# Two of four gate weight slots computed as Strassen block products inside the attention units

## The reference, cut to what matters

```python
q, k, v, qi, ki, wi, u, ga, gb = jnp.split(xn @ w_in, cuts, axis=-1)      # ga, gb: 1024 columns each
m = jax.nn.sigmoid(ga) * (attn_o @ w_branch_attn) + jax.nn.sigmoid(gb) * (pool_o @ w_branch_pool)
h = x + m @ w_out
h = h + moe_ffn(rms_norm(h, ffn_norm_g), ...)                              # 32 experts, top 2
```

## Time and profile before

| what | us |
|---|---|
| median of 3 runs | 1079.64 |
| lowest, highest run | 1079.25, 1081.33 |
| span of the profiled execution (first to last instruction) | 1078.2 |
| PE busy in the span | 948.8 |
| DVE busy | 338.8 |
| ACT busy | 201.7 |
| POOL busy | 196.8 |

### The profile page before, as it was taken

How to read it: one execution, slowest core, us unless ns; L and a number is a source line. 1 busy time by engine, 2 the same in 40 slices (tenths; PEclk the granted TensorE clock), 3 DMA queues, 4 the chain that set the end, 5 groups by cost and what they waited for, 6 DMA issues and landing times.

```text
span 1078.2 us, 12247 instructions
## 1 busy us (share of the span) xinstructions
PE 948.8 (88%) x4745; PEld 534.2 (50%) x4745; DVE 338.8 (31%) x756; ACT 201.7 (19%) x446; POOL 196.8 (18%) x296
## 2 busy tenths in 40 slices
PE   7989999999999999999998999888888877877870
PEld 6644444777676566774553544424334243432420
DVE  3269999965441111330135000000000000000016
ACT  3143110223343334001121000000000000000012
POOL 2740650100001200000231112201111111111122
PEclk9999999999999999999999999999899999999995
DMA  9920211430203832934038999999999999999986
GB/s 341 395 97 1 78 57 68 153 149 18 79 1 138 265 145 69 359 153 156 40 131 322 423 424 422 423 419 426 423 422 424 422 426 421 425 425 423 418 341 208
DMA packets 53690, 283.82 MB, mean 263 GB/s; under 512 B 8684, under 2 KB 9552, under 8 KB 33031
## 3 DMA queue, kind: packets, MB, share of 16 engines
q1 hardware_dynamic: 42807, 246.24, 57.0%
q0 software_dynamic: 10784, 36.97, 9.4%
q10 hardware_dynamic: 56, 0.01, 0.0%
HBM read 267.41 MB, written 23.17 MB: 270 GB/s over the span
## 4 chain that ended last, share of the span: by engine, by line
PE 55%; DMA 26%; DVE 3%; ACT 2%; issue 2%; SPq 1%; POOL 0%; POOLq 0%; ACTq 0%; DVEq 0%
DMA arena<-in_w_exp_up 24%; PE psum L788 11%; PE psum L957 6%; PE psum L626 5%; PE psum L975 5%; PE psum L1063 4%; PE psum L1060 4%; PE psum L1061 4%; PE psum L1080 3%; PE psum L909 1%; DMA y_d<-arena 1%; PE psum L875 1%; PE psum L837 1%; PE psum L859 1%; PE psum L999 1%
## 5 line engine op out<-in xcount | busy, mean ns | idle before, releaser
L1063 PE MATMUL psum<-arena 128*64 128x512 f32 x704 | 164.1, 619 | 28.9 <-DMA arena<-in_w_exp_up 28.2
L1080 PE MATMUL psum<-arena 128*64 128x512 f32 x512 | 116.9, 597 | 17.7 <-ACT arena L1365 17.7
L788 PE MATMUL psum<-arena 128*128 128x288 f32 x480 | 124.6, 412 | 0.0
L1063 PEld LDWEIGHTS psum<-arena 128*64 128x64 f32 x704 | 54.8, 143 | 136.2 <-issue 101.6
L788 PEld LDWEIGHTS psum<-arena 128*128 128x128 f32 x480 | 88.4, 190 | 30.3 <-issue 8.1
L1734 DVE TENSOR_TENSOR arena<-arena,psum 128x256 f32<-128x256 f32 x32 | 13.5, 421 | 274.7 <-ACT arena L1361 274.7
L1361 ACT ACTIVATE arena<-psum 128x256 f32<-128x256 f32 x32 | 12.3, 383 | 402.8 <-PE psum L1063 270.5
L626 PE MATMUL psum<-arena 128*128 128x512 f32 x192 | 84.5, 594 | 0.2 <-ACT arena L1232 0.2
L1080 PEld LDWEIGHTS psum<-arena 128*64 128x64 f32 x512 | 40.4, 136 | 72.1 <-issue 71.4
L1060 PE MATMUL psum<-arena 128*64 128x256 f32 x320 | 56.8, 413 | 15.3 <-DMA arena<-in_w_exp_up 15.3
L1742 DVE COPY arena<-psum 128x512 f32<-128x512 f32 x31 | 21.4, 692 | 152.2 <-PE psum L1080 152.2
(11 more groups left out here) (291 smaller groups left out, 1090.0 us busy)
## 6 DMA issues: line engine op xcount, KB each, us to landing
arena<-in_w_exp_down SPq DMA_DIRECT2D x32, 2048.0 KB, 36.9
arena<-in_w_exp_gate SPq DMA_DIRECT2D x29, 2048.0 KB, 32.3
arena<-in_w_exp_up SPq DMA_DIRECT2D x19, 2048.0 KB, 37.2
arena<-in_w_exp_up SPq DMA_DIRECT2D x26, 1024.0 KB, 33.4
arena<-in_w_in SPq DMA_DIRECT2D x7, 2048.0 KB, 8.8
y_d<-arena SPq DMA_DIRECT2D x1, 8192.0 KB
arena<-in_w_exp_gate SPq DMA_DIRECT2D x6, 1024.0 KB, 13.9
arena<-in_x_prompt SPq DMA_DIRECT2D x8, 512.0 KB, 8.2
```

The source lines that it names most:

```text
L788: last = pe.matmul(bank(2 + n % 2 if n < SAMPLE_G else 2, HN), ring[slot % 2][:, k, m * P:(m + 1) * P], xnT[:, k, HN * hh:HN * hh + HN], s ...
L1063: last = pe.matmul(bank(2 + s, 512, rows).rearrange("p (w n) -> p w n", w=2), x_k, wgu[j][:, :, DE * k + 256 * q:DE * k + 256 * q + 256], ...
L1080: last = pe.matmul(bank(4 + s, 512, slice(64 * half, 64 * half + 64)), hT[s][:, k % 2, CAP * (k // 2):CAP * (k // 2) + CAP], wd[j][:, k, 5 ...
```

## The change

Slots 4 and 5 (gate products 8 to 23, 16 products of 8 matmuls) are computed in another way. A slot's 1024 by 512 weights are taken as pairs of 128-column blocks (`lo`, `hi`), each with an upper and a lower half of the 1024 rows; the tokens as a left and a right half. Each pair is one 2 by 2 block product, done with seven block products of 4 matmuls in place of eight (Strassen's scheme in its form with 15 sums). There are four such pairs (`q` = 0 to 3), so 28 products `g` of 4 matmuls. The sums of weight quarters (`asum`, 4 for each pair, 512 columns; one of them written over the slot itself) and of input quarters (`tsum`, 4 in all, 1152 columns) are made by POOL. `fast_product` issues a product into bank 2 or 3 by turns, and some products accumulate onto what their bank holds from an earlier one. `take_fast` on DVE copies out or adds each result, 28 in place of 16.

In units 0 and 1 PE issues gate products 6 and 7 as before; in units 2 to 15 it issues two fast products in a row at the place of the one gate product, and DVE takes the two of unit u-1 in its round `u`, at the place of the one copy. The numbering of fills is f = n below 8, f = 8 + g for the fast ones, and 36 to 43 for gate products 24 to 31, which now fill the eight places in the sample stage. Nothing is left of the gates behind attention, so the branch products come first there. The sigmoids run in another order, and DVE waits for them tile by tile. POOL makes the input sums and the first weight sums before its first gather of keys, the other three sets of weight sums between it and the first gather of values, and that gather waits for `g_done` 36 (the end of the fast products), because `vb` shares its space with the sums. A slot of `ring` is free again after 8, 22, 36, 44, 60 and 76 products.

```diff
+        gb_raw = [at(ZB - 2 * NT, NT), at(MP, NT), at(ZB - NT, NT), at(GAR + 4 * NT, NT)] + [at(QZ + k * NT, NT) for k in range(4)]
+        assert NT <= 5 * P and GAR + 5 * NT <= MP and QZ + 4 * NT <= KT1
+        QUAD = 4 * HN
+        tsum = [at(ZB + 4096 + j * QUAD, 4, HN) for j in range(3)] + [at(ZB + 8192, 4, HN)]
+        asum = {1: at(SMALL, 4, P), 2: at(where["expand"][0], 4, P), 4: at(ZB + 4096 + 3 * QUAD, 4, P)}
...
-        RING_USED = [(S["jp"], v) for v in (10, 15, 20)] + [(S["g_done"], v) for v in (8, 16, 24, 32, 48, 64)]
-
-        PRE, SAMPLE_G = 6, 22
-        EARLY = SAMPLE_G + DB
-        assert PRE <= 8 and EARLY <= 32 and EARLY - 16 <= 2 * len(gb_raw)
+        RING_USED = [(S["jp"], v) for v in (10, 15, 20)] + [(S["g_done"], v) for v in (8, 22, 36, GATES, GATES + 16, GATES + 32)]
+
+        PRE, SAMPLE_G = 6, 24
+        assert PRE <= 8 and SAMPLE_G + DB == 32
+
+        def fill_of(n):
+            return n if n < 8 else FILLS + n - SAMPLE_G
+
+        def fast_places(g):
+            q, step = g // 7, g % 7
+            slot, pair = R_GATES + 1 + q // 2, q % 2
+            tiles = sgA[4:8] if q < 2 else gb_raw[0:4]
+            return slot, pair, step, tiles[pair], tiles[2 + pair]
...
+                f = fill_of(n)
...
-                    if n >= 2:
-                        pe.wait_ge(S["raw_ev"], n - 1 if n <= SAMPLE_G else n)
+                    if f >= 2:
+                        pe.wait_ge(S["raw_ev"], f - 1 if n <= SAMPLE_G else f)
...
+            def fast_product(g):
+
+                slot, pair, step, _, _ = fast_places(g)
+                f, w = 8 + g, ring[slot % 2]
+                lo, hi = slice(pair * P, pair * P + P), slice((2 + pair) * P, (3 + pair) * P)
+                left, right = slice(0, HN), slice(HN, NT)
+                if step == 0:
+                    ring_ready(slot)
+                if step == 1:
+                    pe.wait_ge(S["sums_t"], 1)
+                    pe.wait_ge(S["sums_a"], 2 * (g // 7) + 1)
+                if step == 6:
+                    pe.wait_ge(S["sums_a"], 2 * (g // 7) + 2)
+                pe.wait_ge(S["raw_ev"], f - 1)
+                a, b = ((w[:, 0:4, lo], xnT[:, 0:4, left]), (asum[2], tsum[1]), (w[:, 4:8, lo], xnT[:, 4:8, left]), (w[:, 0:4, hi], tsum[2]),
+                        (asum[1], tsum[0]), (w[:, 4:8, hi], tsum[3]), (asum[4], xnT[:, 4:8, right]))[step]
+                for k in range(4):
+                    last = pe.matmul(bank(2 + f % 2, HN), a[:, k, :], b[:, k, :], start=(k == 0 and step in (0, 1, 4)), stop=(k == 3), skip_group_check=True)
+                last.then_inc(S["g_done"], 1)
...
-                    gate_part(PRE + u, 0, KD)
+                    if PRE + u < 8:
+                        gate_part(PRE + u, 0, KD)
+                    else:
+                        for g in (2 * (PRE + u - 8), 2 * (PRE + u - 8) + 1):
+                            fast_product(g)
...
-            for p3 in range(3):
-                slot = R_GATES + 3 + p3
+            n = 0
+            for p3 in range(2):
+                slot = R_GATES + 4 + p3
...
-                        if p3 == 0:
-                            b = g_bank()
-                            for k in range(KD):
-                                last = pe.matmul(bank(b, HN), w[:, k, m * P:(m + 1) * P], xnT[:, k, tc], start=(k == 0), stop=(k == KD - 1))
...
-            act.wait_ge(S["raw_ev"], EARLY)
+            act.wait_ge(S["raw_ev"], GATES)
             act.wait_ge(S["son_done"], DB // 2)
-            for k in range(len(gb_raw)):
+            act.activation(sgA[0], sgA[0], ACT.Sigmoid).then_inc(S["gs_done"], 1)
+            for k in range(KD):
                 act.activation(sgB[k], gb_raw[k], ACT.Sigmoid).then_inc(S["gs_done"], 1)
-            for k in range(KD):
+            for k in range(1, KD):
                 act.activation(sgA[k], sgA[k], ACT.Sigmoid).then_inc(S["gs_done"], 1)
-            for n in range(EARLY, 32):
-                act.wait_ge(S["g_done"], n + 1)
-                act.activation(sgB[(n - 16) // 2][:, HN * (n % 2):HN * (n % 2) + HN], bank(4 + (n - EARLY) % 4, HN), ACT.Sigmoid).then_inc(S["gate_ev"], 1)
...
+            def take_fast(g):
+
+                _, _, step, upper, lower = fast_places(g)
+                left, right = slice(0, HN), slice(HN, NT)
+                if g == 0:
                     dve.wait_ge(S["rope_done"], len(JOBS))
                     for s in range(2):
                         dve.wait_ge(s_rs[s], stored[s])
-                dve.wait_ge(S["g_done"], n + 1)
-                dst = sgA[4 * (n // 8) + m] if n < 16 else gb_raw[(n - 16) // 2]
-                dve.tensor_copy(dst[:, cols_h], bank(2 + n % 2 if n < SAMPLE_G else 2, HN)).then_inc(S["raw_ev"], 1)
+                dve.wait_ge(S["g_done"], 8 + g + 1)
+                src = bank(2 + g % 2, HN)
+                if step == 0:
+                    ins = dve.tensor_copy(lower[:, left], src)
+                elif step == 2:
+                    ins = dve.tensor_copy(upper[:, left], src)
+                else:
+                    dst, old = ((upper[:, right], lower[:, left]), None, (lower[:, right], lower[:, left]), (lower[:, right], lower[:, right]),
+                                (lower[:, left], lower[:, left]), (upper[:, right], upper[:, right]))[step - 1]
+                    dve.wait_ge(S["raw_ev"], 8 + g)
+                    ins = dve.tensor_tensor(dst, src, old, ALU.add)
+                ins.then_inc(S["raw_ev"], 1)
...
-                    take_gate(PRE + v)
+                    if PRE + v < 8:
+                        take_gate(PRE + v)
+                    else:
+                        for g in (2 * (PRE + v - 8), 2 * (PRE + v - 8) + 1):
+                            take_fast(g)
...
-                dve.wait_ge(S["gs_done"], KD + len(gb_raw))
-                if mg:
-                    dve.wait_ge(S["gate_ev"], 32 - EARLY)
                 for m in range(4):
+                    dve.wait_ge(S["gs_done"], 1 + len(gb_raw) + 4 * mg + m)
...
+            def left_sums(q):
+
+                slot, pair = R_GATES + 1 + q // 2, q % 2
+                w = ring[slot % 2]
+                lo, hi = slice(pair * P, pair * P + P), slice((2 + pair) * P, (3 + pair) * P)
+                if q:
+                    pool.wait_ge(S["g_done"], 8 + 7 * (q - 1) + 5)
+                pool.wait_ge(s_ring[slot % 2], RING_AT[slot])
+                link(pool.tensor_tensor(asum[1], w[:, 0:4, hi], w[:, 4:8, hi], ALU.add))
+                pool.tensor_tensor(w[:, 0:4, hi], w[:, 0:4, lo], w[:, 0:4, hi], ALU.subtract)
+                pool.tensor_tensor(asum[2], asum[1], w[:, 0:4, lo], ALU.subtract).then_inc(S["sums_a"], 1)
+                if q:
+                    pool.wait_ge(S["g_done"], 8 + 7 * q)
+                pool.wait_ge(S["sums_a"], 2 * q + 1)
+                pool.tensor_tensor(asum[4], w[:, 4:8, lo], asum[2], ALU.subtract).then_inc(S["sums_a"], 1)
+
+            x11, x12, x21, x22 = (xnT[:, 4 * kh:4 * kh + 4, HN * nh:HN * nh + HN] for kh in range(2) for nh in range(2))
+            link(pool.tensor_tensor(tsum[0], x12, x11, ALU.subtract))
+            pool.tensor_tensor(tsum[2], x22, x12, ALU.subtract)
+            link(pool.tensor_tensor(tsum[1], x22, tsum[0], ALU.subtract))
+            pool.tensor_tensor(tsum[3], x21, tsum[1], ALU.subtract).then_inc(S["sums_t"], 1)
+            left_sums(0)
             for bp in range(DB // 2):
                 if bp:
                     pool.wait_ge(S["tp"], T0 + 32 + 11 * (bp - 1) + 8)
@@ -1897,6 +1958,10 @@
                     gather(kb[:, b2, :], k_groups, gidx[:, 2 * bp + b2:2 * bp + b2 + 1], s_kin[b2])
                 if bp:
                     pool.wait_ge(S["spv_done"], bp)
+                else:
+                    for q in range(1, 4):
+                        left_sums(q)
+                    pool.wait_ge(S["g_done"], FILLS)
                 for b2 in range(2):
                     gather(vb[:, b2, :], v_groups, gidx[:, 2 * bp + b2:2 * bp + b2 + 1], s_vin[b2])
                 if bp == 0:
```

More of the change, by code:

```diff
@@ L277, in program @@
         sgA = [at(BANDS + k * NT, NT) for k in range(4)] + [at(GAR + k * NT, NT) for k in range(4)]
-        gb_raw = [at(ZB - 2 * NT + k * NT, NT) for k in range(2)] + [at(MP, NT)] + [at(QZ + k * NT, NT) for k in range(4)]
-        assert NT <= 5 * P
+        gb_raw = [at(ZB - 2 * NT, NT), at(MP, NT), at(ZB - NT, NT), at(GAR + 4 * NT, NT)] + [at(QZ + k * NT, NT) for k in range(4)]
[3 more added lines that the diff above has]
+        asum = {1: at(SMALL, 4, P), 2: at(where["expand"][0], 4, P), 4: at(ZB + 4096 + 3 * QUAD, 4, P)}
+        assert 3 * QUAD + 4 * P <= 4096 and where["expand"][1] >= 4 * P and QUAD <= 2 * LS
         pgi = arena[0:DB, XNT - 80:XNT - 80 + NPAGE].bitcast(I32)
@@ L392, in program @@
         OV, N0 = M[0], NE // 2
+        FILLS = 8 + 28
+        GATES = FILLS + 8
         RING_LOADS = [w_in_v[:, :, c:c + 512] for c in (C_Q, C_K, C_U)]
@@ L488, in _ @@
             load_ring(8)
```

(36 more changed lines are left out.)

4 lines of the change are left out of this document (2 added, 2 removed).

## The result

The changed kernel takes 1124.29 us (median of 4 runs, 1123.86 to 1126.53) against 1080.04 before (4 runs, 1079.25 to 1081.33). The ratio is 1.0412, 95% interval 1.0400 to 1.0425, so 44.3 us slower. The profiled execution is the slowest of the four runs (1126.53); its span is 1125.0 us, 46.8 more than before, so what follows from its rows comes out some 2 us above the medians.

What follows compares the result with a forecast made beforehand. PE's own stream was taken to bound the prompt units, and weight DMA the expert stage. -7.8 + 35 + 10.9 = +38 on the span of 1078.2 gave 1116, with the runs' offset 1117.7, stated as 1117 us; range 1105 to 1127.

Steps and rivals of the forecast that it cites:

- the likeliest case (A): Prompt units: all terms as summed, clock falling after 4 to 13 gaps; 1113 to 1128 us, chance 0.60.
- Term 1: Behind attention: the last two gate products, 32 matmul records, go from PE's path; -7.8 us.
- so term 1 stands whole: Behind attention: sigmoids, DVE and weight loads keep ahead of the branch products, so the full 7.8 us is gained.
- Term 2: Units 3 to 15: PE waits for DVE to empty a PSUM bank, 13 gaps; +35 us.
- Term 3: Prompt units: PE's clock falls after long gaps, 1.66 us a fall; +10.9 us, bounds 0 and 21.6.
- I take falls in the last eight at 9 of 11: Units 8 to 15: clock falls at the expert stage's rate for long waits, 8 x 0.82 x 1.66 us.
- The upper bound of 21.6: Prompt units: a clock fall of 1.66 us after each of the 13 gaps.
- PE's work in the units is denser: Prompt units: PE's other work is denser than in the expert stage, given for the lower bound of 0 falls.
- POOL's sums and the gathers: Prompt stage: POOL's additions and the moved gathers stay hidden behind other work; cost 0.
- Case C: Prompt units: another wait on top, late values or weight sums, or POOL slowing DVE; 1128 to 1140 us, chance 0.07.
- B: Prompt units: the gaps come but the clock stays, up to 3 falls; 1106 to 1112 us, likeliest 1107, chance 0.26.
- D: Prompt units: not slower, gaps below 0.60 us a unit; down to 1072 us, chance 0.05 faster, 0.02 tie.

Runs made afterwards that it cites:

- e1_same_round: The changed kernel with DVE's two takes moved one round forward, so round u takes unit u's own products: 1072.57 us, ratio 0.9934.
- e7_no_last_gates: The kernel before with gate products 30 and 31 cut from 8 matmuls to 1 each, sigmoids in their old order: 1082.09 us, ratio 1.0016.
- e3_filler: The changed kernel with 3 to 5 unused matmuls of 288 columns in each of the 13 gaps: 1107.16 us, ratio 1.0248.
- e4_before_tight: The kernel before, with gate products 9 to 21 waiting for the take of the product directly before, not two before: 1133.30 us, ratio 1.0486.
- e2_no_sums: The changed kernel without POOL's 20 additions and the waits for them, gate values left wrong: 1126.10 us, ratio 1.0411.
- e5_half: The changed kernel with only the first of a unit's two takes moved into its own round: 1082.23 us, ratio 1.0016.
- e6_one_filler: The changed kernel with one unused matmul of 0.5 us in each of the 13 gaps: 1118.05 us, ratio 1.0347.

## Why the prediction was right, and which term was mis-sized

**Direction and mechanism: right.** Slower by a wait for the PSUM bank was the forecast, and the likeliest case (A) is what came. 1124.3 lies in the range (1105 to 1127), near its upper end, and 7 us over the 1117 named.

**Term 1, -7.8 for the last two gate products: right.** With the gaps gone 7.5 us are left (e1_same_round), and in the changed kernel itself the path shortens by 7.8 behind attention. The step "so term 1 stands whole" rested on the sigmoids' new order; e7_no_last_gates shows that it had to.

**Term 2, +35 for the wait: right.** 33.8 us of idle in the profile, to which the 0.07 for each gap comes by which the profile counts later than I did, 34.7; e3_filler puts it at 34.6 in run time. Thirteen gaps, and unit 2 spared, as worked out. e4_before_tight shows it as the whole cause: the kernel before, without any Strassen product, gets the same gaps by the same wait. The single gaps came within 0.15 us of what the earlier trace rows give (1.96, 2.35, 2.66 and 3.06 as the profile counts), except in unit 4, 0.23 shorter, and in unit 8, 0.55 longer, where POOL held up DVE.

**Term 3, +10.9 for the clock: the mechanism right, the size wrong.** It measured 18.8 in the profiled execution, and 17.1 by the medians (1124.29 - 1107.16, with the gaps filled). The step that failed is in "I take falls in the last eight at 9 of 11": for the last eight units it was nearly right (seven falls for 6.6), but it puts units 3 to 7 at nothing. It read a boundary near 2.57 us of idle out of the expert stage's waits, where the one wait between 1.6 and 2.57 us is the 2.23 of the earlier trace rows. In the units falls came after 1.86, 2.35 and 2.26 too (units 3, 5, 7), 5.0 us; and two of the later falls lasted well into the second product and cost 3.0 us, not 1.66, 2.7 us more. That is the 7.9 us between 10.9 and 18.8 but for 0.2. So the clock was below 1.00 from unit 3 on, not from unit 8 on as forecast, and the stage ended 53 us later, not 45. The upper bound of 21.6 held. The sentence that PE's work in the units is denser, which spoke for fewer falls, found no support: falls came there after four gaps under 2.57 us, and in the expert stage after none. The Trainium skill (TensorE: Matmul & The Clock Gate, psum-queue depth-cycling) says that a kernel which waits for PSUM banks in each iteration can go back and forth between the levels, and the trace agrees: ten falls after thirteen waits. Taken whole it gave 21.6, nearer to the 18.8 than my own term.

**The sum.** -7.8 + 34.7 + 18.8 = 45.7, against 45.4 at the start of the output projection. The medians differ by 44.3; the profiled execution is the changed kernel's slowest run. That 1124.3 fell inside the range is due to its bounds on the falls, not to the 6.6 taken as likeliest.

**POOL's sums and the gathers: right, at 0.** POOL's first and last addition before its first gather, and the first gather of values:

```profile
207.80 2.63 POOL L1949 TENSOR_TENSOR arena<-arena 128x1152 f32<-128x1152 f32 x1 [15.97 <-PE psum L854]
...
222.29 1.09 POOL L1946 TENSOR_TENSOR arena<-arena 128x512 f32<-128x512 f32 x1
```

```profile
373.22 0.96 POOL L1835 DMA_INDIRECT arena<-in_cache_v,arena  x1 [35.39 <-PE psum L825]
```

1152 columns took 2.63 us (2.62 worked out), and the first weight sums end at 223.4, 15 us before unit 2's second product. The value gather at 373.2 leaves 19.5 us to the first value products (392.67), which don't wait. Case C's "DVE's rounds slowed by POOL's work" is real, but 0.7 us once.

**The rivals.** B (the clock stays) is what e3_filler makes by hand: 1107, the number given for it. D fails: the gaps are 1.9 to 3.2 us, not under 0.6. But D named what would have to hold, that DVE takes a product before the next unit's logits, and e1_same_round does just that, at 1072.6 for 1072 worked out.

**What stays open.** Which of the gaps makes the clock fall. It alternates between units 3 to 7 in one way in the changed kernel and in the other in e4_before_tight, after gaps of nearly the same length, and e2_no_sums has falls in units 3, 6 and 7; unit 15's gap of 2.96 us had no fall in either of them, but one in e2_no_sums. No run here separates the length of a gap from its place in time.

## What to carry to other kernels

Where a product is split into two, the buffers it fills turn over twice as fast: look at each wait that counts fills ("the one two before") and ask how much time two fills now are, and where in its own order the engine stands that empties them. Here the arithmetic saving was 7.8 us, a consumer placed one round late took back 35, and moving two lines to the consumer's own round turned 4% slower into 0.7% faster. A gap of PE should be costed at more than its length: in these units every microsecond of gap cost about another half in lost clock (18.8 us on 33.8), and filling idle time that stayed with unused matmuls won 17 us of it back. Gaps of about a microsecond (e5_half) cost only their length.

## What the runs showed of the hardware

- In the units, where gaps came every 8 to 13 us, the granted clock fell after some of well below 2.6 us: 1.67 (e6_one_filler), 1.86 and 2.26 (the changed kernel), for 1.4 to 1.7 us of lost time each, at times 3.0. Other gaps of 1.67 to 2.97 passed without. The gaps of up to 1.16 us in e5_half and the three of up to 1.57 in e6_one_filler never did it. Whether their coming so often matters was not tested.
- Unused matmuls in the gaps kept the clock at 1.00 in all thirteen units and made the kernel 17 us faster.
- A DVE instruction on 2 columns of SBUF (a `TENSOR_SCALAR`) took 0.85 us, not 0.17, while POOL's addition of 512 columns ran, and ended with it; beside POOL's first additions DVE's 1032-column instructions kept their 1.23 and 1.21 us. The Trainium skill (SBUF — State Buffer, section on two separate sides) says that the two engines share a pair of SBUF ports, and that a GpSimd instruction, or a DVE instruction of the kinds that use the pair, holds it for its whole length while the other stands still. The row on 2 columns agrees; the 1032-column rows show no such stop.
